# A two-layer hybrid trunk on one core: first loads in quarters, the norm's sum split and moved, and five smaller edits

## The chip, the cores and the metric

The kernel runs on 1 core of one Trainium2 chip. The metric is the device time of that core in microseconds (us). Before the change it is 975.6 us, the median of 3 runs (975.24 to 975.84). TensorE (PE) multiplies, VectorE (DVE) and ScalarE (ACT) move and compute, SyncE (SP) issues most of the transfers. Each engine works through its own list of instructions in order and waits on semaphores for the others.

## What is computed

The input x is 512 tokens by 1024 channels, float32. Two layers follow each other, each of them

```
h = rmsnorm(x, norm_g)
(qa, ka, va, ga, qb, kb, vb, ab, gb, cq, ckv, kr, gc, mg) = split_cols(h @ w_in)
ya = swa_sink_attention(rope(qa), rope(ka), va) * silu(ga)        # window attention, 8 heads, 2 kv heads
log_a = log_sigmoid(ab @ w_alpha + b_alpha) / 16                  # gate of the linear attention, rank 16
yb = rmsnorm(gla_chunk_readout(qb, kb, vb, log_a)) * silu(gb)     # gated linear attention, 4 heads
q_c, kv = rmsnorm(cq) @ w_uq, rmsnorm(ckv) @ w_ukv                # latent attention, 8 heads
yc = mla_attention(q_c, kv, rope(kr)) * silu(gc)
y = sigmoid(mg)[0] * (ya @ w_oa) + sigmoid(mg)[1] * (yb @ w_ob) + sigmoid(mg)[2] * (yc @ w_oc)
x = x + y @ w_out
```

and a last rmsnorm. The norm of h is not applied to x: only its gain is, and the factor rstd, one per token, is multiplied in when a product leaves PSUM.

## The kernel before

**Pieces.** All weights are packed into 77 pieces per layer of 128 x 1024 numbers (512 KB). A piece passes through three slots: SP loads it into `raw`, ACT rounds it to fp32r in `w_hi` (`split_hi`, L861), DVE subtracts and leaves the rest in `w_lo` (`split_lo`, L1152). A product of x with a piece is three passes on PE (L586): hi by hi, hi by the activation's low part, low by hi. A piece of the kind "ring" gives one 128 x 512 bank out of three from 24 such passes of 512 columns; a "natural" piece (`PN1`, pieces 3 to 6, and `PN2`) adds to four banks `nat` in 24 passes of 432 or 512 columns. The first pieces of a layer are 0 (`PX`, the keys of the window attention), 1 and 2 (`PC[0:2]`, cq), 3 to 6 (`PN1`: kb, va, kr, ab), 7 (`PC[2]`, ckv), 8 and 9 (`PQA`).

**The written order.** `make_schedule` makes one list that PE, ACT and DVE all go through in this order, each doing its own part of every step. A piece is four "quarter" steps (quarter q belongs to piece q // 4). ACT does its part at the last quarter of piece p: `split_hi` of piece p + 3, which takes the slot of piece p and so waits until PE has finished p. DVE does `split_lo` of piece p + 2 at the second quarter of piece p. Between the quarters stand named steps:

- `begin`: the last two of eight squares of x on ACT (`square`, L879) and their sums on DVE (`add`, L1127 and L1130). The first six stand ahead of the layer (for layer 0 behind the splits of the first pieces, ahead of everything else). They use `merged` as room: `sq`, `sq_sum`.
- `rms`: PE multiplies `sq_sum` by a matrix of ones in fp32 (L697), ACT takes Ln and Exp (L866, L868; ahead of them it loads its table, L1002), DVE refines it into `rstd` with four instructions (L1135 to L1143) and scales the rotary tables (L1278, L1279). PE waits here for the four constant loads (`setup_loaded`).
- `early`: DVE empties the banks of pieces 0 to 2 (six instructions, L1285 to L1292); ACT squares the two latent tiles (L986), for which it waits on DVE.
- `rstd_nat` (PE transposes rstd, L702; DVE copies, L1314), `lat_sum` (L1296), `rope_k` (DVE, four instructions, L1302 and L1304).
- at the last quarter of piece 6 DVE takes the 48 columns of kr and ab out of `nat` and rotates kr (`k_ab`, L1496 to L1505); `turn_ab` (PE, L708) transposes the result and waits for it.
- `gla_gate`: PE multiplies `ab1` by `alpha_all` (L714), 17 rows (rank 16 and the bias), from partition 32 on; `gla_decay` (L721) is a product of the same width from 128 rows.

The step `latent` sums squares on PE in fp32r, from a hi and a low part (L735, L736), which ACT and DVE make by a copy (L947) and a subtraction (L1320).

In every layer `rms` stands between piece 2 and piece 3, `early` in the middle of piece 3, `rstd_nat` in the middle of piece 4, `rope_k` in the middle of piece 5, `turn_ab` in the middle of piece 7.

**Window attention.** It is worked off in two halves between quarters of output and gate pieces: `score_a` (L783), `divide_a`, `turn_a` (PE transposes, L817, ACT copies out, L1078), then `value_a` (L831) for each of the four tiles of 128 tokens into the bank `aux`, which DVE gates into `y_pre` (L1165) and ACT and DVE split (`y_hi`, `y_lo`). `score_a(1)` needs the banks that ACT empties at `turn_a(0)`; two quarters lie between them. `value_a(2)` and `value_a(3)` have two quarters around each.

**Latent attention.** Piece `PUKV` gives eight banks of 3 passes; ACT empties the even ones, DVE the odd ones (L1542), and behind them DVE does one `split_lo`. Piece `PUQ` gives three banks of 6 passes. DVE waits for two of them, and then rotates them with L1551 to L1554; the second of these frees the first bank.

**The start.** SP loads x tile by tile with the second halves of pieces 0 and 1 in between, then piece 2, the constants (1.2 MB), and piece 3 and on. ACT's queue loads the first quarter of piece 0, `params`, the first half of piece 1 and the second quarter of piece 0 (`HEADS`). PE runs 7 warming products on zeros (L673), and then pieces 0 and 1 together, k by k (`first_pieces`, L660 to L662): k = 0 and 1 of piece 0, the same of piece 1, then both by turns. ACT splits x (L895) and the parts of the pieces (L902, L913), DVE makes the low parts (L1177, L1182).

Of the kernel before, what the change touches and what calls it, by code (L numbers as in the profile page):

```python
# [17 lines left out]
F32 = mybir.dt.float32  # L18
# [33 lines left out]
WARM = 7  # L52
# [51 lines left out]
def make_schedule():  # L104
# [98 lines left out]
    for y in range(2):  # L203
# [87 lines left out]
def build_hybrid_trunk(nc, x_t, pieces, params, alpha, tables, consts, final_g, out_t, k_rope_dram):  # L291
    with ExitStack() as ctx:
# [85 lines left out]
        o_t = o_bank[:, :].rearrange("p (f n) -> p f n", f=BR)  # L378

# [5 lines left out]
        HEADS = ((0, slice(0, 256)), (1, slice(0, 512)), (0, slice(256, 512)))  # L385
        head_loaded = [sig(f"head_loaded{n}", 0) for n in range(3)]
# [14 lines left out]
        warm_set = sig("warm_set", 0)  # L401
        act_used = sig("act_used", 3, 3)
# [50 lines left out]
        def _(sp):  # L453
            for j in range(KT):
                sp.dma_start(xt[:, j, :], x_t[:, j, :]).then_inc(x_loaded[j].sem, 16)
                if j in (3, 4):
                    sp.dma_start(raw[:, j - 3, 512:1024], pieces[j - 3, :, 512:1024]).then_inc(raw_loaded[j - 3].sem, 16)
            sp.dma_start(raw[:, 2, :], pieces[2]).then_inc(raw_loaded[2].sem, 16)
            sp.dma_start(rope[:, :, :], tables).then_inc(setup_loaded.sem, 16)
            sp.dma_start(con[:, :], consts).then_inc(setup_loaded.sem, 16)  # L460
            sp.dma_start(alpha_all[32:32 + B_RANK + 1, :, :], alpha).then_inc(setup_loaded.sem, 16)
            sp.dma_start(fin_g[:, :], final_g).then_inc(setup_loaded.sem, 16)
            for n in range(RAW, DEPTH * PIECES):
# [41 lines left out]
        def _(pe):  # L505
# [140 lines left out]
            def first_pieces():  # L646

                jobs = [(p, k) for p in range(2) for k in range(2)] + [(p, k) for k in range(2, KT) for p in range(2)]
                for p, k in jobs:
                    if k == 0:  # L650
                        pe.wait_ge(proj_free.sem, proj_free.at(0, p - 2))
                        pe.wait_ge(head_lo.sem, p + 1)
                    elif (p, k) == (0, 2):
                        pe.wait_ge(head_lo.sem, 3)
# [4 lines left out]
                    hi, lo = w_hi[:, p, k * P:(k + 1) * P], w_lo[:, p, k * P:(k + 1) * P]  # L659
                    pe.matmul(ring[p][:, :], hi, act_hi[:, k, :], start=k == 0, stop=False)  # L660
# [1023 lines left out]
```

## Time and profile before

| | |
|---|---|
| time, median of 3 runs | 975.6 us (975.24 to 975.84) |
| the profiled execution: its own time | 975.85 us |
| its span in the trace | 974.0 us |
| PE busy | 963.5 us, 99% |
| DVE busy | 578.0 us, 59% |
| ACT busy | 402.5 us, 41% |
| chain that ended last | PE 91%, DVE 5%, ACT 3% |
| granted TensorE clock, mean | 0.999 |

A row of the timeline gives the start, the duration, the engine, the line, the operation, its operands (out<-in) and the count; in brackets stands how long the engine had sat idle and what ended that. Products overlap: a pass of 512 columns lasts 0.39 us in its row, and the next starts 0.227 us after it, so PE's time is read from one start to the next. The same holds for DVE and ACT, where an instruction that waits for nothing can start up to 0.1 us before the end that the row ahead of it gives.

### The profile page before, as it was taken

The numbers are of one execution on the slowest core, as the hardware profiler recorded it, in microseconds if no ns is written. First come the engines' busy times: TensorE is split into PE (matmuls) and PEld (weight loads), VectorE is DVE, ScalarE is ACT, GpSimd is POOL, SyncE is SP. The second block draws the span as 40 slices with busy tenths as digits, with TensorE's granted clock in tenths as the row PEclk, the third lists the DMA queues.
The fourth block names the chain that finished last, engine by engine and source line by source line (L and its number), as shares of the span: only waits on it lengthen the run. The fifth ranks groups of instructions, "written<-read, shape, count | busy, mean of one in ns | idle before, by whom it ended". The sixth has DMA issues, their size and how long they took to land.

```text
span 974.0 us, 13475 instructions
## 1 busy us (share of the span) xinstructions
PE 963.5 (99%) x5440; PEld 787.7 (81%) x5440; DVE 578.0 (59%) x944; ACT 402.5 (41%) x766; POOL 0.9 (0%) x5
## 2 busy tenths in 40 slices
PE   8999999999999999999999999999999999999997
PEld 6878888888888877788888888888888887777887
DVE  6856466346647565665556654744574666665844
ACT  6443343225533354532435324431363424544334
POOL 0000000000000000000000000000000000000000
PEclk9999999999999999999999999999999999999999
DMA  7324313322125221122223333233222341111212
GB/s 269 121 78 139 109 65 109 108 87 87 66 66 161 87 66 66 45 85 88 92 82 108 121 102 115 75 98 104 73 76 93 103 128 66 66 63 47 94 59 87
DMA packets 29968, 91.38 MB, mean 94 GB/s; under 512 B 4353, under 2 KB 6913, under 8 KB 29778
## 3 DMA queue, kind: packets, MB, share of 16 engines
q1 hardware_dynamic: 28770, 89.25, 27.4%
q10 hardware_dynamic: 1136, 1.27, 0.5%
q8 instruction: 43, 0.70, 0.3%
q14 instruction: 19, 0.16, 0.0%
HBM read 84.67 MB, written 2.23 MB: 89 GB/s over the span
## 4 chain that ended last, share of the span: by engine, by line
PE 91%; DVE 5%; ACT 3%; DMA 1%; issue 1%; ACTq 0%; DVEq 0%
PE ring L586 72%; PE nat L586 5%; PE nat L803 3%; PE aux L845 2%; PE nat L810 2%; DVE w_lo L1152 1%; ACT work L1058 1%; PE aux L831 1%; DMA raw<-pieces 1%; ACT w_hi L861 1%; PE nat L783 0%; PE ring L607 0%; PE nat L714 0%; PE ring L608 0%; PE ring L609 0%
## 5 line engine op out<-in xcount | busy, mean ns | idle before, releaser
L586 PE MATMUL ring<-act_hi,w_hi 128*128 128x512 f32 x832 | 330.3, 397 | 0.0
L586 PE MATMUL ring<-act_hi,w_lo 128*128 128x512 f32 x832 | 324.4, 390 | 0.0
L586 PE MATMUL ring<-act_lo,w_hi 128*128 128x512 f32 x832 | 324.2, 390 | 0.0
L861 ACT ACTIVATE w_hi<-raw 128x1024 fp32r<-128x1024 f32 x152 | 161.2, 1062 | 390.4 <-PE ring L586 359.4
L1152 DVE TENSOR_TENSOR w_lo<-raw,w_hi 128x1024 fp32r<-128x1024 f32 x152 | 185.2, 1220 | 50.9 <-ACT w_hi L861 50.9
L586 PEld LDWEIGHTS ring<-act_hi,w_hi 128*128 128x128 f32 x832 | 156.2, 188 | 37.3 <-issue 6.3
L586 PEld LDWEIGHTS ring<-act_hi,w_lo 128*128 128x128 f32 x832 | 156.2, 188 | 33.3
L586 PEld LDWEIGHTS ring<-act_lo,w_hi 128*128 128x128 f32 x832 | 156.3, 188 | 30.5
L1474 DVE SCALAR_TENSOR_TENSOR gates<-ring,rstd 128x512 f32<-128x512 f32 x72 | 49.7, 691 | 140.8 <-PE ring L586 140.8
L586 PE MATMUL ring<-y_hi,w_lo 128*128 128x512 f32 x192 | 74.7, 389 | 0.0
L586 PE MATMUL ring<-y_lo,w_hi 128*128 128x512 f32 x192 | 74.7, 389 | 0.0
L586 PE MATMUL ring<-y_hi,w_hi 128*128 128x512 f32 x192 | 74.7, 389 | 0.0
L586 PE MATMUL nat<-w_hi,act_hi 128*128 128x512 f32 (+1 forms) x128 | 48.8, 381 | 0.4 <-DVE w_lo L1152 0.3
L999 ACT ACTIVATE gates<-gates 128x512 f32<-128x512 f32 x72 | 44.8, 623 | 10.1 <-DVE gates L1474 10.1
L586 PE MATMUL nat<-w_lo,act_hi 128*128 128x512 f32 (+1 forms) x128 | 47.8, 374 | 0.0
L586 PE MATMUL nat<-w_hi,act_lo 128*128 128x512 f32 (+1 forms) x128 | 47.8, 373 | 0.0
L1070 ACT ACTIVATE work<-nat,neg_top 128x128 f32<-128x128 f32 (+3 forms) x64 | 32.9, 526 | 34.9 <-DVE neg_top L1422 34.9
L586 PEld LDWEIGHTS ring<-y_hi,w_hi 128*128 128x128 f32 x192 | 36.0, 188 | 7.5
L586 PEld LDWEIGHTS ring<-y_lo,w_hi 128*128 128x128 f32 x192 | 36.0, 188 | 7.5
L586 PEld LDWEIGHTS ring<-y_hi,w_lo 128*128 128x128 f32 x192 | 36.0, 188 | 7.4
L1524 DVE SCALAR_TENSOR_TENSOR gates<-gates,ring 128x512 f32<-128x512 f32 x32 | 22.0, 687 | 14.8 <-PE ring L586 14.8
L803 PE MATMUL nat<-bank_g,bank_a 32*128 32x128 f32 (+3 forms) x384 | 30.4, 445 | 0.0
(219 smaller groups left out, 998.9 us busy)
## 6 DMA issues: line engine op xcount, KB each, us to landing
raw<-pieces SPq DMA_DIRECT2D x152, 512.0 KB, 3.5
xt<-x_t SPq DMA_DIRECT2D x8, 256.0 KB, 6.9
bank_a<-work SPq DMA_DIRECT2D x32, 64.0 KB, 2.0
out_t<-gates SPq DMA_DIRECT2D x7, 256.0 KB, 2.3
rope<-tables SPq DMA_DIRECT2D x1, 1024.0 KB
bank_a<-work SPq DMA_DIRECT2D x32, 32.0 KB, 2.0
raw<-pieces SPq DMA_DIRECT2D x2, 256.0 KB, 7.3
bank_g<-k_rope_dram SPq DMA_DIRECT2D x8, 64.0 KB, 3.2
```

The source lines that it names most:

```text
L586: mm = pe.matmul(dst, stationary, moving, start=start and i == 0, stop=stop and i == 2)
L803: mm = pe.matmul(nat[a][:, 0:n], q, k, start=part == 0, stop=part == 2)
L810: mm = pe.transpose(nat[a][:, b * P:(b + 1) * P], prob[a][:, b * P:(b + 1) * P], ident)
L831: mm = pe.matmul(o_t[r * 64:r * 64 + 64, 2 * h:2 * h + 2, c * 64:c * 64 + 64], (v_as, v_a)[c][:, i, h * A_DH:(h + 1) * A_DH], pt[:, r, c], ...
L845: mm = pe.matmul(o_t[r * 64:r * 64 + 64, f, :], v_c[:, b, h * C_V:(h + 1) * C_V], prob_t[h % 4][:, b * P:(b + 1) * P], start=b == 0, stop= ...
L861: nc.scalar.activation(w_hi[:, n % HL, :], raw[:, n % RAW, :], ACT.Copy).then_inc(hi_split.sem, 1)
L999: nc.scalar.activation(gates[:, j if j >= 4 else 8 + j, :], gates[:, j, :], ACT.Tanh).then_inc(gate_tanh.sem, 1)
L1058: one = nc.scalar.activation(prob[k][:, hh * P:(hh + 1) * P], nat[k][:, hh * P:(hh + 1) * P], ACT.Exp, scale=A_SCALE, bias=neg_top[:, qt % ...
L1070: nc.scalar.activation(prob[a][:, 0:n], nat[a][:, 0:n], ACT.Exp, scale=C_SCALE, bias=neg_top[:, i % 2, a:a + 1], accum_out=sums[:, qt, 4 * ...
L1152: nc.vector.tensor_tensor(w_lo[:, n % HL, :], raw[:, n % RAW, :], w_hi[:, n % HL, :].bitcast(F32), ALU.subtract).then_inc(lo_split.sem, 1)
L1474: nc.vector.scalar_tensor_tensor(gates[:, j, :], res, 0.5, rstd[:, :], ALU.mult, ALU.mult).then_inc(proj_free.sem, 1)
L1524: nc.vector.scalar_tensor_tensor(merged[:, j, :] if b == 0 else tile, tile, 1.0, z, ALU.add, ALU.mult).then_inc(proj_free.sem, 1)
```

## The change

- **Start.** `WARM` goes from 7 to 4. The first halves of pieces 0 and 1 are loaded in four quarters (`HEADS`): two on ACT's queue behind `params`, two on SP's behind the third tile of x. ACT's wait for `params` moves behind the first split. In `first_pieces` the three passes of a k are ordered hi by hi, low by hi, hi by low activation, each with its own wait ahead of it. SP loads piece 3 ahead of the constants, behind a wait for the low part of piece 0.
- **Squares.** In layer 0 all eight squares and sums stand behind the splits of piece 3 (ACT: last quarter of piece 0; DVE: second quarter of piece 1).
- **rms.** It moves from behind piece 2 to behind piece 3, in both layers; `early`, `rstd_nat`, `lat_sum` move on by about a piece; `rope_k` moves by half a piece only; `turn_ab` and `gla_gate` stay. The sum is taken in fp32r: ACT copies `sq_sum` to `lat_hi[:, 1]`, DVE subtracts into `lat_lo[:, 1]`, PE makes two passes in place of the fp32 product.
- **alpha.** `alpha_all` and `ab1` have all 128 rows, zeros in the rows without a weight; its load grows from 34 KB to 256 KB.
- **Window attention.** Three quarters in place of two behind `turn_a(0)`. The values of tiles 2 and 3 are one step, `values_a`, the second into `nat[0]`; `gate_a` gates them one after the other.
- **Latent attention.** DVE's `split_lo` of `PUKV` stands behind its first copy in place of behind its last; in `PUQ` DVE starts on the first bank before it waits for the second.

```diff
-WARM = 7
+WARM = 4
     piece(PX, PC[0], PC[1])
+    piece(PN1[0])
     step(("rms", 0))
-    half(PN1[0], 0)
+    half(PN1[1], 0)
     step(("early", 0))
-    half(PN1[0], 1)
-    half(PN1[1], 0)
-    step(("rstd_nat", 0), ("lat_sum", 0))
     half(PN1[1], 1)
     half(PN1[2], 0)
+    step(("rstd_nat", 0), ("lat_sum", 0))
+    half(PN1[2], 1)
     step(("rope_k", 0))
-    half(PN1[2], 1)
     piece(PN1[3])
     half(PC[2], 0)
     step(("turn_ab", 0))
...
-        quarters(2 - y)
+        quarters(3 - 2 * y)
     todo.append(("y_hi", 1))
     quarters(1)
+    todo.append(("y_lo", 1))
+    todo.append(("values_a", 2))
     for y in range(2, TT):
-        todo.append(("y_lo", y - 1))
-        todo.append(("value_a", y))
+        todo.append(("gate_a", y))
         quarters(1)
         todo.append(("y_hi", y))
         quarters(1)
-    todo.append(("y_lo", TT - 1))
+        todo.append(("y_lo", y))
...
-        HEADS = ((0, slice(0, 256)), (1, slice(0, 512)), (0, slice(256, 512)))
+        HEADS = ((0, slice(0, 256)), (1, slice(0, 256)), (0, slice(256, 512)), (1, slice(256, 512)))
...
                 sp.dma_start(xt[:, j, :], x_t[:, j, :]).then_inc(x_loaded[j].sem, 16)
-                if j in (3, 4):
+                if j == 2:
+                    for n in range(2, 4):
+                        p, cols = HEADS[n]
+                        sp.dma_start(raw[:, p, cols], pieces[p, :, cols]).then_inc(head_loaded[n].sem, 16)
+                elif j in (3, 4):
                     sp.dma_start(raw[:, j - 3, 512:1024], pieces[j - 3, :, 512:1024]).then_inc(raw_loaded[j - 3].sem, 16)
             sp.dma_start(raw[:, 2, :], pieces[2]).then_inc(raw_loaded[2].sem, 16)
+            sp.wait_ge(lo_split.sem, 1)
+            sp.dma_start(raw[:, 0, :], pieces[RAW]).then_inc(raw_loaded[0].sem, 16)
             sp.dma_start(rope[:, :, :], tables).then_inc(setup_loaded.sem, 16)
             sp.dma_start(con[:, :], consts).then_inc(setup_loaded.sem, 16)
-            sp.dma_start(alpha_all[32:32 + B_RANK + 1, :, :], alpha).then_inc(setup_loaded.sem, 16)
+            sp.dma_start(alpha_all[:, :, :], alpha).then_inc(setup_loaded.sem, 16)
...
                     if k == 0:
                         pe.wait_ge(proj_free.sem, proj_free.at(0, p - 2))
+                        pe.wait_ge(head_hi.sem, p + 1)
+                    elif k == 2:
+                        pe.wait_ge(head_hi.sem, p + 3)
+                    elif k == KT // 2:
+                        pe.wait_ge(hi_split.sem, hi_split.at(0, p + 1))
+                    if p == 0:
+                        pe.wait_ge(x_hi.sem, x_hi.at(0, k + 1))
+                    hi, lo = w_hi[:, p, k * P:(k + 1) * P], w_lo[:, p, k * P:(k + 1) * P]
+                    pe.matmul(ring[p][:, :], hi, act_hi[:, k, :], start=k == 0, stop=False)
+                    if k == 0:
                         pe.wait_ge(head_lo.sem, p + 1)
...
+                    pe.matmul(ring[p][:, :], lo, act_hi[:, k, :], start=False, stop=False)
                     if p == 0:
                         pe.wait_ge(x_lo.sem, x_lo.at(0, k + 1))
-                    pe.matmul(ring[p][:, :], hi, act_hi[:, k, :], start=k == 0, stop=False)
-                    pe.matmul(ring[p][:, :], hi, act_lo[:, k, :], start=False, stop=False)
-                    mm = pe.matmul(ring[p][:, :], lo, act_hi[:, k, :], start=False, stop=k == KT - 1)
+                    mm = pe.matmul(ring[p][:, :], hi, act_lo[:, k, :], start=False, stop=k == KT - 1)
...
# PE, rms
-                        pe.wait_ge(x_acc.sem, x_acc.at(layer, LATE))
-                        mm = pe.matmul(aux[:, :], ones, sq_sum, start=True, stop=True)
+                        pe.wait_ge(sum_lo.sem, sum_lo.at(layer, 1))
+                        pe.matmul(aux[:, :], ones_r[:, :], lat_hi[:, 1, :], start=True, stop=False)
+                        mm = pe.matmul(aux[:, :], ones_r[:, :], lat_lo[:, 1, :], start=False, stop=True)
# PE, gla_gate
-                            mm = pe.matmul(nat_gate[:, t, :], ab1[32:32 + B_RANK + 1, t * P:(t + 1) * P],
-                                           alpha_all[32:32 + B_RANK + 1, layer, :], start=True, stop=True)
+                            mm = pe.matmul(nat_gate[:, t, :], ab1[:, t * P:(t + 1) * P], alpha_all[:, layer, :],
+                                           start=True, stop=True)
# PE
+                    elif name == "values_a":
+                        pe.wait_ge(turn_out.sem, turn_out.at(layer, 8))
+                        pe.wait_ge(o_read.sem, o_read.at(layer, i))
+                        value_a(i, o_t).then_inc(value_done.sem, 1)
+                        value_a(i + 1, o_t2).then_inc(value_done.sem, 1)
# ACT, quarters
+                        if (layer, p) == (0, PX):
+                            first_squares()
# ACT, rms
+                        act.wait_ge(x_acc.sem, x_acc.at(layer, LATE))
+                        nc.scalar.activation(lat_hi[:, 1, :], sq_sum, ACT.Copy).then_inc(sum_hi.sem, 1)
                         nc.scalar.preload_act_table_set(LN_EXP)
# DVE, rms
+                        dve.wait_ge(sum_hi.sem, sum_hi.at(layer, 1))
+                        nc.vector.tensor_tensor(lat_lo[:, 1, :], sq_sum, lat_hi[:, 1, :].bitcast(F32),
+                                                ALU.subtract).then_inc(sum_lo.sem, 1)
# DVE, quarters
                             split_lo(layer, i // 4 + 2)
+                            if (layer, i) == (0, 5):
+                                first_sums()
# DVE, PUKV and PUQ
-                            split_lo(layer, p + 2)
+                                if o == 1:
+                                    split_lo(layer, p + 2)
...
-                                evacuated(layer, p, 2)
+                                evacuated(layer, p, 1)
                                 nc.vector.tensor_tensor(work[:, 0, :], ra, cos, ALU.mult)
                                 nc.vector.tensor_tensor(work[:, 3, :], ra, sin, ALU.mult).then_inc(proj_free.sem, 1)
+                                evacuated(layer, p, 2)
```

## Rows read from the trace of the kernel before

**Rows 1.** The page, part 1: busy time, share of the span and instructions of TensorE.
```profile
PE 963.5 (99%) x5440; PEld 787.7 (81%) x5440; DVE 578.0 (59%) x944; ACT 402.5 (41%) x766; POOL 0.9 (0%) x5
```
**Rows 2.** The warming line: count, durations min/median/max in ns, first and last start.
```profile
L673 PE MATMUL aux<-merged x14: 379/606/767, 1.7 to 6.3; 128*128 128x256 f32 x14
```
**Rows 3.** The page, part 2: transfer rate of 40 equal slices of the span.
```profile
GB/s 269 121 78 139 109 65 109 108 87 87 66 66 161 87 66 66 45 85 88 92 82 108 121 102 115 75 98 104 73 76 93 103 128 66 66 63 47 94 59 87
```
**Rows 4.** Timeline of PE at the start: start, us, engine, line, operation, [idle before].
```profile
7.31 0.47 PE L660 MATMUL ring<-act_hi,w_hi 128*128 128x512 f32 x1 [0.62 <-DVE act_lo L1177]
...
9.80 0.47 PE L660 MATMUL ring<-act_hi,w_hi 128*128 128x512 f32 x1 [0.86 <-DVE w_lo L1182]
...
19.56 0.39 PE L586 MATMUL ring<-act_hi,w_hi 128*128 128x512 f32 x1
```
**Rows 5.** Timeline of ACT at the start.
```profile
5.35 0.42 ACT L902 ACTIVATE w_hi<-raw 128x256 fp32r<-128x256 f32 x1 [1.43 <-DMA par_all<-params]
5.67 1.32 ACT L895 ACTIVATE act_hi<-xt,par_all 128x512 fp32r<-128x512 f32 x2
8.30 0.63 ACT L902 ACTIVATE w_hi<-raw 128x512 fp32r<-128x512 f32 x1 [1.31 <-DMA raw<-pieces]
```
**Rows 6.** Timeline of PE in layer 1, from rms to turn_ab.
```profile
502.12 1.02 PE L697 MATMUL aux<-merged,ones_r 128*128 128x512 f32 x2
...
503.18 0.35 PE L586 MATMUL nat<-w_hi,act_lo 128*128 128x432 f32 x1
...
510.02 0.49 PE L702 MATMUL aux<-con,rstd 128*128 128x128 f32 x3
...
517.92 0.47 PE L586 MATMUL nat<-w_hi,act_hi 128*128 128x432 f32 x1 [0.26 <-DVE w_lo L1152]
...
525.57 0.49 PE L708 MATMUL aux<-con,gates 128*48 128x128 f32 x3
```
**Rows 7.** Timeline of ACT and DVE: a split, a copy and a subtraction in a row.
```profile
51.92 1.06 ACT L861 ACTIVATE w_hi<-raw 128x1024 fp32r<-128x1024 f32 x1 [1.62 <-PE ring L586]
52.89 0.61 ACT L947 ACTIVATE lat_hi<-merged 128x512 fp32r<-128x512 f32 x1
...
53.53 0.69 DVE L1320 TENSOR_TENSOR lat_lo<-merged,lat_hi 128x512 fp32r<-128x512 f32 x1 [0.97 <-ACT lat_hi L947]
```
**Rows 8.** Timeline: a sum in fp32r on PE and ACT's Ln behind it.
```profile
70.20 0.40 PE L735 MATMUL aux<-lat_hi,ones_r 128*128 128x512 f32 x1
...
70.87 0.69 ACT L866 ACTIVATE merged<-aux,eps 128x512 f32<-128x512 f32 x1 [1.62 <-PE aux L736]
```
**Rows 9.** Timeline of ACT and DVE in layer 1, from the norm's Ln to k_ab.
```profile
504.75 0.69 ACT L866 ACTIVATE merged<-aux,eps 128x512 f32<-128x512 f32 x1
...
506.13 0.69 DVE L1135 TENSOR_TENSOR y_pre<-rstd 128x512 f32<-128x512 f32 x1 [6.88 <-ACT rstd L868]
...
525.21 0.22 DVE L1505 TENSOR_TENSOR gates<-gates 128x64 f32<-128x64 f32 x1
```
**Rows 10.** Timeline of PE around gla_gate.
```profile
51.44 0.39 PE L586 MATMUL ring<-act_hi,w_lo 128*128 128x512 f32 x1
51.76 1.99 PE L714 MATMUL nat<-alpha_all,merged 17*128 17x256 f32 x8
53.68 0.50 PE L586 MATMUL ring<-act_hi,w_hi 128*128 128x512 f32 x1
```
**Rows 11.** Timeline of PE in the window attention.
```profile
239.75 0.34 PE L783 MATMUL nat<-bank_a 64*64 64x128 f32 x4 [0.57 <-ACT bank_a L1078]
...
260.50 0.50 PE L586 MATMUL ring<-act_hi,w_hi 128*128 128x512 f32 x1
...
263.44 0.66 PE L831 MATMUL aux<-work,bank_a 128*64 128x128 f32 x8
```
**Rows 12.** Timeline of DVE and PE at piece PUQ.
```profile
289.91 2.35 DVE L1152 TENSOR_TENSOR w_lo<-raw,w_hi 128x1024 fp32r<-128x1024 f32 x2
...
293.61 0.47 PE L586 MATMUL ring<-lat_hi,w_hi 128*128 128x512 f32 x1 [0.26 <-DVE work L1552]
```

More of the change, by code:

```diff
@@ L667, in aux_bank, with value_a @@
                 pe.wait_ge(aux_free.sem, aux_free.at(layer, u))
+            def value_a(i, bank):
+                for h in range(A_KV):
+                    pt = prob_t[2 * (i % 2) + h].rearrange("p (a r c n) -> p r c a n", a=2, r=2, c=2)
+                    for c in range(2):
+                        for r in range(2):
+                            mm = pe.matmul(bank[r * 64:r * 64 + 64, 2 * h:2 * h + 2, c * 64:c * 64 + 64],
+                                           (v_as, v_a)[c][:, i, h * A_DH:(h + 1) * A_DH], pt[:, r, c], start=True, stop=True)
+                return mm
             pe.wait_ge(warm_set.sem, 1)
@@ L793, in _ @@
                         if i == 0:
+                            pe.wait_ge(o_read.sem, o_read.at(layer, TT))
                             pe.wait_ge(proj_free.sem, proj_free.at(layer, by_dve(first_output(PUQ + 2))))
@@ L879, in square @@
                 nc.scalar.activation(sq[n % 2], xt[:, (n - 1 - LATE) % KT, :], ACT.Square).then_inc(x_sq.sem, 1)
-            for n, (p, cols) in enumerate(HEADS):
+            act.dma_start(par_all[:, :, :], params).then_inc(par_loaded.sem, 16)
+            for n in range(2):
+                p, cols = HEADS[n]
                 act.dma_start(raw[:, p, cols], pieces[p, :, cols]).then_inc(head_loaded[n].sem, 16)
-                if n == 0:
-                    act.dma_start(par_all[:, :, :], params).then_inc(par_loaded.sem, 16)
             nc.scalar.preload_act_table_set(LN_EXP)
-            act.wait_ge(par_loaded.sem, 16)
             def split_x(layer, j):
@@ L914, in _, with first_squares @@
             split_hi(0, 2)
-            for n in range(LATE + 1, LATE + 1 + ACT_TILES):
-                square(-1, n, buffer_used=n > LATE + 2)
+            def first_squares():
+                for n in range(LATE + 1, LATE + 1 + ACT_TILES):
+                    square(-1, n, buffer_used=n > LATE + 2)
+                for n in range(1, LATE + 1):
+                    square(0, n)
             for layer in range(DEPTH):
@@ L920, in _ @@
                     if name == "begin":
-                        for n in range(1, LATE + 1):
-                            square(layer, n)
+                        if layer > 0:
+                            for n in range(1, LATE + 1):
+                                square(layer, n)
                     elif name == "split_x" and layer + 1 < DEPTH:
@@ L1187, in _ @@
                 split_x(0, j)
-                if j == 1:
-                    for n in range(1, 3):
+                if j in (1, 2):
+                    for n in ((1,) if j == 1 else (2, 3)):
                         dve.wait_ge(head_hi.sem, n + 1)
@@ L1195, in _, with first_sums @@
             split_lo(0, 2)
-            for n in range(LATE + 1, KT + 1):
-                tile = n - 1 - LATE
-                if tile < ACT_TILES:
-                    dve.wait_ge(x_sq.sem, tile + 1)
-                else:
-                    dve.wait_ge(x_loaded[tile].sem, 16)
-                    dve.wait_ge(x_acc.sem, x_acc.at(-1, n - 2))
-                    nc.vector.tensor_tensor(sq[n % 2], xt[:, tile, :], xt[:, tile, :], ALU.mult
-                                            ).then_inc(dve_sq.sem, 1)
-                    dve.wait_ge(dve_sq.sem, tile - ACT_TILES + 1)
-                add(-1, n)
+            def first_sums():
+                for n in range(LATE + 1, KT + 1):
+                    tile = n - 1 - LATE
+                    if tile < ACT_TILES:
+                        dve.wait_ge(x_sq.sem, tile + 1)
+                    else:
+                        dve.wait_ge(x_loaded[tile].sem, 16)
+                        dve.wait_ge(x_acc.sem, x_acc.at(-1, n - 2))
+                        nc.vector.tensor_tensor(sq[n % 2], xt[:, tile, :], xt[:, tile, :], ALU.mult
+                                                ).then_inc(dve_sq.sem, 1)
+                        dve.wait_ge(dve_sq.sem, tile - ACT_TILES + 1)
+                    add(-1, n)
+                for n in range(1, LATE + 1):
+                    add_square(0, n)
             def add_half(m):
@@ L1665 @@
         params[:, l, SINKS:SINKS + A_HEADS] = a_sinks[l][None, :]
+    rows = np.zeros((P, DEPTH, B_HEADS * B_DK), x.dtype)
+    rows[32:32 + B_RANK] = w_alpha.transpose(1, 0, 2)
+    rows[32 + B_RANK] = b_alpha
     arrays = {
@@ L1669 @@
         "params": params,
-        "alpha": np.ascontiguousarray(np.concatenate([w_alpha, b_alpha[:, None, :]], axis=1).transpose(1, 0, 2)),
+        "alpha": rows,
         "tables": rotary_tables(),
```

34 lines of the change are left out of this document (16 added, 18 removed).

## The prediction, as put on record before the run

> **What bounds the kernel now.** I read, in this order: the page's busy times, PE's gaps from start to start in the timeline, who ended each gap, and then the timelines of ACT and DVE around the steps that move. The page shows TensorE busy for 963.5 of 974.0 us [rows 1]; the reader is to see that whatever is won or lost must be a gap on PE or a pass on PE. Other engines cost nothing until PE waits for them. So each edit is priced by what PE does at its place: a gap that closes, a pass that goes, or a new wait whose chain through ACT and DVE is longer than the work that PE has in between. The few gaps that the change touches are at the start, 7.31 and 9.80 us [rows 4], at a natural piece behind `early`, 517.92 [rows 6], ahead of `score_a(1)`, 239.75 [rows 11], and in `PUQ`, 293.61 [rows 12].
>
> The sum is made against the profiled execution (975.85 us, span 974.0). The median of the three runs is 975.6, 0.25 less; I take the difference found and add it to the median.
>
> **The rms step, both layers: the largest term.** `rms` now stands behind piece 3. At the last quarter of piece 3 ACT has `split_hi` of piece 6, which takes piece 3's slot and so waits until PE has finished piece 3. Behind it in ACT's list stands the new copy of the sum, then DVE's subtraction, and only then may PE's first pass start; PE has nothing else to do, since its list is in order too. The length of this chain is in the trace piece by piece:
> - from the moment at which PE could start its next pass to ACT's split: the last pass ahead of `gla_gate` starts at 51.44 [rows 10], so the next could at 51.67, and ACT starts at 51.92 [rows 7]: 0.25 us;
> - split, then copy: 52.89 - 51.92 = 0.97; copy, then subtraction: 53.53 - 52.89 = 0.64; subtraction 0.69 [rows 7];
> - DVE's end to PE's start: 525.21 + 0.22 = 525.43 against 525.57 [rows 6, 9]: 0.14.
>
> Together 2.7 us of idle PE per layer. Before, PE needed only DVE's sum here, which was long done. Bounds: 2.3 if a copy can start sooner behind the split, 3.1 if in layer 0 the postponed squares make ACT or DVE late. I find them in time: ten DVE instructions of about 0.7 us [rows 9] are 7 us from the split of piece 3 on, while pieces 2 and 3 take 5.4 and 4.7, and the subtraction is not due before ACT's copy; splits 4 and 5 fit in until then.
>
> **From rms to turn_ab, both layers.** DVE's list between these two is a chain that just fitted before: its last `k_ab` instruction ends at 525.43 and PE's transposes start at 525.57 [rows 6, 9]. Now PE has a piece less between the two, DVE only a split less. Counted from the start S of rms:
> - PE: 525.57 - 502.12 = 23.45 before [rows 6]. A natural piece goes, 24 passes at (510.02 - 503.18) / 35 = 0.195, which is 4.69. The gap at 517.92 goes, 0.26 idle and about 0.15 of slow restart, 0.41. The fp32 product took 503.18 - 502.12 - 0.20 = 0.86; two fp32r passes take 2 x 0.23 = 0.46; 0.40 less. PE is there at S + 17.95.
> - ACT and DVE: Ln starts 70.87 - 70.20 = 0.67 behind S [rows 8], the refinement 506.13 - 504.75 = 1.38 behind Ln, the end of `k_ab` 525.43 - 506.13 = 19.30 behind that [rows 9], less one split of piece weights, 2.35 - 1.22 = 1.13 [rows 12]. With 0.14 to PE: S + 20.36.
>
> So PE stands at `turn_ab` for 2.4 us. DVE's list is in order: `early`, the wait for ACT's squares and split 7, `rope_k`, split 8 all stand ahead of `k_ab`. Bounds 1.9 and 2.9. Behind `turn_ab` all steps keep their distances.
>
> From the end of piece 2 to `turn_ab` it was 23.45; it becomes 4.69 + 2.70 + 20.36 = 27.75: **4.3 us more per layer, 8.6 in all**, with the gain of the shorter sum and of the closed gap already in it.
>
> **The start.** Before, pieces 0 and 1 took from 7.31 to 19.56 [rows 4]: 48 passes at 0.227 are 10.9, the rest is the gap ahead of 9.80 (about 1.0: six passes end near 8.75) and restarts. The first pass waited for act_lo; now it needs only the high part of tile 0, which ACT starts at 5.67 and has by about 6.35 [rows 5]: first pass near 6.45. `params` goes first and the weights' quarter behind it, so that the first split still starts near 5.3, as both together landed then [rows 5]. The gap at 9.80 waited for a half piece that landed at 8.30 [rows 5] as the end of the first 404 KB of its queue (128, 20 and 256); the quarter that takes its place is the end of the first 276 KB. At the rate between the two landings (256 KB in 3 us) that is 6.8, with both splits done near 8.1. By then PE has done five or six passes and stands briefly twice. 42 passes remain from about 8.2: end near 17.75. **1.8 us less.** Bounds: 0.8 (the quarter lands no sooner than 8.0) and 2.6 (no gap behind 6.45). Constants and piece 3, 2 MB, are now issued behind the first low part, at about 11 us; at the 269 GB/s of the first slice [rows 3] they take 7 to 8 us, and rms is at 30.
>
> The three warming products less cost nothing if the clock stays up: they go from a stretch that ended ahead of the first piece, with 0.62 idle behind it [rows 4].
>
> **Alpha.** The entry to `gla_gate` takes 51.76 - 51.44 = 0.32 where 0.23 is usual, and the eight records 53.68 - 51.76 = 1.92 [rows 10]; by the fp32 product of 512 columns in 0.86, four of 256 would take 1.72. A full-height product may save up to 0.29, or nothing; I take 0.2, since both comparisons point the same way. **0.4 less in two layers.** By the Trainium skill (TensorE: Matmul & The Clock Gate, step by step: what each phase is for), loading weights scales with columns while the number of rows does not matter; by that rule alone this edit would give 0 and the time would be 0.4 higher. The trace has the extra 0.09 and 0.20, but not what they come from.
>
> **Window attention.** PE sat 0.57 idle at `score_a(1)`, with the restart 0.65 [rows 11]; one more quarter, six passes or 1.36 us, covers it. 1.3 in two layers (1.1 to 1.3). Joining two value steps takes out one change of tile shape around a run of 12 passes: 263.44 - 260.50 = 2.94 against 12 x 0.227 = 2.72, 0.22 [rows 11], and I add 0.1 for the second step's own entry, an estimate: 0.6 in two layers (0.4 to 0.8). The joined step waits for ACT's four copies of about 0.6, which start during the transposes and have 2.94 us of passes behind these.
>
> **PUQ.** The gap at 293.61 is 0.26 idle, 0.4 with the restart [rows 12]: DVE did two splits (2.35) ahead of emptying the first bank. One of them moves into `PUKV`, where DVE's copies come 1.36 us apart and a copy of 0.6 with a split of 1.13 do not fit into that; the third bank may come 0.15 late. I take 0.25 per layer, **0.5**, between -0.2 and 0.8.
>
> **Sum:** 8.6 - 1.8 - 0.4 - 1.3 - 0.6 - 0.5 = 4.0 us slower: 979.85 against the profiled 975.85, **979.6** as a median. With all ends of the terms together 1.9 to 6.9 us slower, that is 977.5 to 982.5.
>
> **Rivals.**
> - *Only the rms wait counts.* If DVE reaches `k_ab` 2.4 us sooner relative to rms (because ACT's `early` squares stop holding split 7), the turn is hidden: 979.6 - 4.8 = 974.8. For it: the gap at 517.92 shows a split that came late there [rows 6]. Against: `k_ab` ended 0.14 ahead of the transposes, with nothing to spare [rows 6, 9], and the change takes away 4.7 us of PE's work and 1.1 of DVE's.
> - *Both waits are covered, the gains stay: faster.* Place: `rms`. It decides when the copy is done as PE ends piece 3, which would need ACT's split of piece 6 not to wait for piece 3. Then there is no 2.7, and with S earlier but DVE's chain already running, no 2.4: 975.6 - 4.6 - 2 x 0.81 = 969.4. Against: slot 6 mod 3 is slot 3 mod 3.
> - *The clock falls.* With 4 products of 0.71 on average the warming ends near 5 and PE is idle for over a us and patchy until 8.2. Its records run from 767, with a median of 606, down to 379 ns [rows 2], the two levels, 1.2 and 2.4 GHz. Eight passes at the lower one would take 0.2 longer each, 1.6: 981.3. If it also fell behind the stalls of 2.7 and 2.4, up to 6 more. For it: such long gaps do not occur before. Against: after the gap of 0.86 at 9.80 passes ran at full rate [rows 4]. The Trainium skill (TensorE: Matmul & The Clock Gate, what's actually happening) has an idle engine fall to half rate and a busy one return; by that rule short gaps like these would leave the clock up.
>
> **How the numbers follow.** Forecast with both waits: 0.66. Clock rival 0.10. Only the rms wait 0.13. Both covered 0.08, with 0.03 for other mishaps. A measurement of this kernel tells from no change what is over 0.2%, 2 us; 973.65 to 977.55 is "same". Slower: the forecast almost whole and the clock, 0.76; same: the first rival and an edge of the forecast, 0.16; faster 0.08. The forecast alone spans 977.5 to 982.0; the range for 8 in 10 reaches down to the first rival: 974.7 to 982.2.
>
> **What would show it.** PE's row at rms idle for some 2.3 us with DVE's subtraction as its releaser, in both layers; ACT's split of piece 6 and the copy right ahead of it; PE's row at `turn_ab` idle for about 2 us, released by `k_ab`; first piece done near 17.75; no idle at `score_a(1)`. It is wrong if PE passes rms without a gap, or if the first pieces end later than 19.

## The result, and the profile after

| | before | after |
|---|---|---|
| median of 6 runs each, us | 975.72 (975.24 to 976.18) | 980.02 (979.50 to 981.49) |
| profiled execution, own time / span, us | 975.85 / 974.0 | 981.49 / 979.7 |
| PE busy, us | 963.5 | 963.4 |
| end of pieces 0 and 1, us | 19.56 | 19.55 |
| end of piece 2 to `turn_ab`, layer 0 / layer 1, us | 23.47 / 23.46 | 27.83 / 27.84 |
| mean granted clock | 0.999 | 0.997 |

The ratio is 1.0045, 95% interval 1.0035 to 1.0056: slower by 0.35 to 0.56%. The forecast was 979.6.

PE is as busy as before [rows 1]; what the kernel lost is idle time. The first part of after's page, busy time by engine:
```profile
PE 963.4 (98%) x5434; PEld 790.0 (81%) x5434; DVE 579.4 (59%) x947; ACT 403.1 (41%) x769; POOL 0.9 (0%) x5
```
The list of PE's waits of after (line, releaser: us in total, times, longest; the one ahead of the warming is left out) shows where: two waits per layer that before did not have, one for the split of the sum of squares and one for `k_ab`.
```profile
PE aux L724 <- DVE lat_lo L1322: 5.1, 2, 2.5
PE aux L736 <- DVE gates L1556: 3.3, 2, 2.4
...
PE ring L668 <- ACT act_hi L921: 0.9, 1, 0.9
```
**The row norm.** Layer 1 of after, timeline of ACT and DVE, answers to [rows 7, 9]. In order: the split of piece 6, the copy of the sum behind it, a table load, DVE's subtraction, Ln, and the last instruction of `k_ab`.
```profile
509.67 1.06 ACT L888 ACTIVATE w_hi<-raw 128x1024 fp32r<-128x1024 f32 x1 [3.64 <-PE nat L594]
510.64 0.61 ACT L1041 ACTIVATE lat_hi<-merged 128x512 fp32r<-128x512 f32 x1
511.27 1.28 ACT L1042 ACT_TABLE_LOAD   x1
...
511.28 0.69 DVE L1322 TENSOR_TENSOR lat_lo<-merged,lat_hi 128x512 fp32r<-128x512 f32 x1 [3.99 <-ACT lat_hi L1041]
...
512.86 0.69 ACT L893 ACTIVATE merged<-aux,eps 128x512 f32<-128x512 f32 x1 [0.31 <-PE aux L725]
...
532.19 0.22 DVE L1556 TENSOR_TENSOR gates<-gates 128x64 f32<-128x64 f32 x1
```
PE in the same stretch of layer 1, with `turn_ab` of layer 0 as the first line; it answers to [rows 6]:
```profile
52.83 0.60 PE L736 MATMUL aux<-con,gates 128*48 128x128 f32 x4 [2.42 <-DVE gates L1556]
...
509.22 0.36 PE L594 MATMUL nat<-w_lo,act_hi 128*128 128x432 f32 x1
512.12 0.47 PE L724 MATMUL aux<-lat_hi,ones_r 128*128 128x512 f32 x1 [2.54 <-DVE lat_lo L1322]
...
512.85 0.54 PE L594 MATMUL nat<-w_hi,act_lo 128*128 128x432 f32 x1
513.19 0.56 PE L594 MATMUL nat<-w_lo,act_hi 128*128 128x432 f32 x1
...
532.56 0.60 PE L736 MATMUL aux<-con,gates 128*48 128x128 f32 x4 [0.88 <-DVE gates L1556]
```
Read the pairs of starts. From the last pass of piece 3 to the first of the norm it is 512.12 - 509.22 = 2.90, of which the pass itself is 0.195: 2.70 lost. From there to `turn_ab` it is 20.44. Behind the stall the passes of layer 1 start 0.36 apart instead of 0.195: PE runs at the lower of its two levels, 1.2 GHz. The windows of after (us, busy time and number by engine, then the granted clock, DMA share, GB/s) show it as 0.61 for 4 us:
```profile
512.00:516.00 4.00, 3.88 (x12) 3.57 (x13) 1.69 (x3) 1.87 (x3) 0.00 (x0) 0.61 0.00 0
516.00:520.00 4.00, 4.00 (x21) 3.82 (x21) 3.92 (x7) 0.00 (x0) 0.00 (x0) 0.97 0.01 2
```
It costs nothing here: `turn_ab` waits for DVE in any case. The slow passes took 1.5 us more, and the idle time at `turn_ab` is shorter by just that, 0.88 instead of 2.42. So both layers have the same 27.8 between the same two points.

**The start.** PE of after, answers to [rows 4]. The first pass starts 1.0 sooner than before, but the passes start 0.43 apart, and full rate begins only at 11.12.
```profile
6.30 0.76 PE L668 MATMUL ring<-act_hi,w_hi 128*128 128x512 f32 x1 [0.86 <-ACT act_hi L921]
...
10.71 0.58 PE L675 MATMUL ring<-act_hi,w_lo 128*128 128x512 f32 x1
11.12 0.39 PE L678 MATMUL ring<-act_lo,w_hi 128*128 128x512 f32 x1
```
**`gla_gate`** of after, answers to [rows 10]:
```profile
56.04 1.89 PE L742 MATMUL nat<-alpha_all,merged 128*128 128x256 f32 x8
57.57 0.59 PE L594 MATMUL ring<-act_hi,w_hi 128*128 128x512 f32 x1
```
The step from its first product to the next piece takes 1.53, before 1.92; from `turn_ab` to `gla_decay`, whose work is the same otherwise, 13.15 (52.83 to 65.98) against 13.52 (48.47 to 61.99). A short window of the timeline starts its row at the first record that falls into it. So it gives the starts of the second and of the last of the eight, before and then after:
```profile
52.08 1.02 PE L714 MATMUL nat<-alpha_all,merged 17*128 17x256 f32 x4
53.37 0.37 PE L714 MATMUL nat<-alpha_all,merged 17*128 17x256 f32 x1
...
56.25 1.02 PE L742 MATMUL nat<-alpha_all,merged 128*128 128x256 f32 x4
57.54 0.38 PE L742 MATMUL nat<-alpha_all,merged 128*128 128x256 f32 x1
```
From the second record to the last it is 1.29 with 17 rows and 1.29 with 128. The difference is at the two ends of the run of products. From the pass ahead of it to the second record it is 0.64 before (from 51.44) and 0.44 after (from 55.81). From the last record to the second pass behind it, it is 0.64 before (to 54.01) and 0.46 after (to 58.00). Together that is 0.38.

The ledger of the two profiled spans, after less before: +4.36 and +4.38 between piece 2 and `turn_ab`; start 0.0; per layer alpha -0.37, the window quarter -0.65, the joined value step -0.36; `PUQ` -0.36 in layer 0 and nothing in layer 1, where the restart ahead of it still takes 0.25. That is 8.7 - 3.1 = 5.6, and the spans differ by 5.7. The profiled execution of after is the longest of its six, 1.5 over their median. In which place the others are shorter no trace shows. An earlier rise of the clock at the start would give part of it: copy_first and old_order, with the same warming and first loads, reached full rate some 1.5 us sooner and ended the two pieces 0.7 and 0.6 sooner than after. That it was so in the other executions of after is argued only.

### The profile page after: what moved, and what is told of

The parts are those of the page before. It is cut to its first block, busy times and chain, and to the rows that moved or that the text cites. A ratio compares the mean times of both kernels' runs of the same rounds, so it can differ in the third digit from the quotient of the medians.

```text
span 979.7 us, 13470 instructions
## 1 busy us (share of the span) xinstructions
PE 963.4 (98%) x5434; PEld 790.0 (81%) x5434; DVE 579.4 (59%) x947; ACT 403.1 (41%) x769; POOL 0.9 (0%) x5
## 3 DMA queue, kind: packets, MB, share of 16 engines
q1 hardware_dynamic: 29184, 89.74, 27.8%
## 4 chain that ended last, share of the span: by engine, by line
PE 94%; DVE 4%; ACT 1%; issue 1%; DMA 0%; ACTq 0%; DVEq 0%
PE ring L594 74%; PE nat L594 5%; PE nat L832 3%; PE aux L872 2%; PE nat L839 2%; DVE w_lo L1192 1%; PE nat L811 1%; PE nat L846 1%; PE aux L692 1%; PE ring L668 0%; PE ring L675 0%; PE ring L678 0%; ACT w_hi L888 0%; PE ring L615 0%; DMA raw<-pieces 0%
```

## Experiments

The kernels of the first four ran on one chip, beside before at 975.55 (975.23 to 976.66, 15 runs); those of the last three on another, beside before at 975.80 (974.93 to 976.38, 21 runs). Their medians are given with the ratio to before. The measure that tells the theories apart is the stretch from the end of piece 2 to `turn_ab`, read from each timeline. All values are in us:

| kernel | end of pieces 0, 1 | piece 2 to `turn_ab`, layer 0 | layer 1 | median |
|---|---|---|---|---|
| before | 19.56 | 23.47 | 23.46 | 975.7 |
| after | 19.55 | 27.83 | 27.84 | 980.02 |
| warm7 | 18.36 | 28.33 | 27.84 | 980.12 |
| copy_first | 18.83 | 27.03 | 27.02 | 982.47 |
| copy_rope | 19.76 | 24.18 | 24.18 | 973.76 |
| small_four | 20.41 | 23.47 | 23.46 | 972.52 |
| old_order | 18.97 | 26.65 | 25.24 | 977.05 |
| warm4_before | 19.89 | 23.47 | 23.46 | 976.16 |
| best | 17.80 | 23.46 | 23.47 | 971.28 |

**warm7.** After, with the warming of before.
```diff
-WARM = 4
+WARM = 7
```


> The changed kernel with WARM = 7 again, all else as changed. Theory (the clock): with four warming products TensorE stayed at half rate until 11.1 us, eleven passes at 0.43 in place of 0.227; with seven it is at full rate when the first piece starts, so pieces 0 and 1 end near 17.8 us in place of 19.55 and the time falls from 980.0 to about 978.3. Rival (the slow passes come from the order of the passes or from the loads, not from the warming): they stay slow until 11 us, pieces 0 and 1 end near 19.5, 980.0.

Measured 980.12 (979.78 to 981.06), ratio 1.0046 (1.0033 to 1.0059). This is the rival's time, but not for the rival's reason. Timeline of PE:
```profile
7.24 0.58 PE L668 MATMUL ring<-act_hi,w_hi 128*128 128x512 f32 x1
7.66 0.40 PE L675 MATMUL ring<-act_hi,w_lo 128*128 128x512 f32 x1
```
The passes run at full rate from 7.66 on and the two pieces end 1.2 sooner than in after, so the slow passes did cost that much. The first pass is 0.9 later than in after, since the seven products, nearly all of them at the lower level, last until it. Then the stall of 2.54 at the norm took the clock down in layer 0 as well, and here the norm's own two products ran slow: the second starts 0.57 behind the first where after has 0.30, Ln and all behind it come later, and the stretch is 28.33. Of the 1.2 there are 0.7 left: the profiled spans are 979.0 and 979.7. The medians show none of it.

**copy_first.** The copy of the sum and its subtraction become a step of their own ahead of the last quarter of piece 2, so that no split that waits for piece 3 stands before them.
```diff
-    piece(PX, PC[0], PC[1])
+    piece(PX, PC[0])
+    half(PC[1], 0)
+    step(("quarter", 4 * PC[1] + 2), ("sum", 0), ("quarter", 4 * PC[1] + 3))
...
# ACT and DVE: the copy and the subtraction
-                    elif name == "rms":
+                    elif name == "sum":
...
```


> The changed kernel, with the copy and the subtraction of the norm's sum as a step of their own one quarter before the end of piece 2, ahead of ACT's splits of pieces 5 and 6. Theory (the rms wait is ACT's order): in layer 1 TensorE passes rms without idling, in layer 0 it waits 0.7 us for the late squares instead of 2.5; the wait at turn_ab stays at 2.4 us in both layers, counted from rms; 980.0 - 2.7 - 2.0 = 975.3. Rival (what limits is the chain from the norm to turn_ab as a whole and not ACT's order): the idle time only moves from rms to turn_ab, 980.0.

Measured 982.47 (981.07 to 983.08), ratio 1.0066 (1.0052 to 1.0080). That is above both expectations, and above after too, by 2.4 in the medians and by 0.5 in the profiled spans. PE's waits of this kernel:
```profile
PE aux L738 <- DVE gates L1559: 7.0, 2, 3.5
...
PE ring L596 <- DVE w_lo L1195: 0.6, 1, 0.6
PE aux L726 <- DVE lat_lo L1324: 0.6, 1, 0.6
```
The wait at the norm is gone in layer 1 and is 0.6 in layer 0 (before the edit 2.5 in both), and the one at `turn_ab` grew from 2.4 to 3.5. ACT of layer 1 shows what I had not priced; PE's product is there at 509.19:
```profile
509.45 1.06 ACT L890 ACTIVATE w_hi<-raw 128x1024 fp32r<-128x1024 f32 x1 [3.64 <-PE nat L596]
510.53 1.28 ACT L1045 ACT_TABLE_LOAD   x1
511.83 0.69 ACT L895 ACTIVATE merged<-aux,eps 128x512 f32<-128x512 f32 x1
```
In after the split and the table load run beside the stall, and Ln starts 0.74 behind the product. Here both stand between the product and Ln, which starts 2.64 behind it. The end of `k_ab` moves only from 27.69 to 26.9 behind piece 2, so of the 2.7 that leave the norm in layer 1 only 0.8 are kept, and the rest turns into waits further on. Behind the stall of 3.49 the passes start 0.43 apart, with no further wait to absorb it. From `turn_ab` to the end of piece 2 of layer 1 this kernel takes 1.3 more than after (453.20 for 451.89), and from `turn_ab` of layer 1 to the end of the span 1.5 more (448.7 for 447.1). With 0.7 less at the start and 0.8 less in each stretch that is the 0.5 between the profiled spans, 980.2 and 979.7. The medians stand 2.4 apart, and where the other 1.9 lie no trace shows.
```profile
51.30 1.02 PE L738 MATMUL aux<-con,gates 128*48 128x128 f32 x4 [3.49 <-DVE gates L1559]
...
52.54 0.63 PE L596 MATMUL ring<-act_lo,w_hi 128*128 128x512 f32 x1
52.97 0.63 PE L596 MATMUL ring<-act_hi,w_lo 128*128 128x512 f32 x1
```
**copy_rope.** As copy_first, and in addition `rope_k` stands behind `turn_ab`, so that its instructions leave DVE's list ahead of `k_ab`.
```diff
-    step(("rope_k", 0))
     piece(PN1[3])
     half(PC[2], 0)
-    step(("turn_ab", 0))
+    step(("turn_ab", 0), ("rope_k", 0))
...
```


> As copy_first, and rope_k moved behind turn_ab, so that DVE has 2.85 us less ahead of k_ab. Theory (turn_ab waits for DVE's list): no idle at turn_ab, k_ab ends some 0.5 us ahead of the transposes; 975.3 - 4.8 = 970.5. Rival (k_ab waits for something else, for example for piece 6 or for ACT): the wait at turn_ab stays, 975.3.

Measured 973.76 (972.33 to 974.38), ratio 0.9978 (0.9969 to 0.9986). PE's waits:
```profile
PE aux L737 <- DVE gates L1558: 1.3, 2, 0.6
PE ring L595 <- DVE w_lo L1194: 0.6, 1, 0.6
PE aux L725 <- DVE lat_lo L1323: 0.6, 1, 0.6
```
The stretch falls to 24.18. That is 2.85 less than in copy_first, the time of the four instructions that moved (46.85 to 49.70 in layer 0 of after), and 3.7 less than in after, in each layer; the kernel is 6.3 faster than after. DVE's list, which is worked off in order, was what held `turn_ab`. The time is 3.3 above the expectation. The two stretches gave 7.3 where the expectation had 9.5, since `turn_ab` still waits 0.63 and 0.64 and a split of layer 1 0.65, and the two pieces end 0.2 later, at 19.76. The remaining 0.9 is again the difference between profiled executions (7.1 apart) and medians (6.3 apart).

**small_four.** Before, with the four small edits and nothing else: alpha at full height, the window quarter, the joined value step, `PUKV` and `PUQ`.
```diff
-        quarters(2 - y)
+        quarters(3 - 2 * y)
...
+    todo.append(("values_a", 2))
...
-        todo.append(("value_a", y))
+        todo.append(("gate_a", y))
...
-  mm = pe.matmul(nat_gate[:, t, :], ab1[32:32 + B_RANK + 1, ...], alpha_all[32:32 + B_RANK + 1, layer, :], ...)
+  mm = pe.matmul(nat_gate[:, t, :], ab1[:, ...], alpha_all[:, layer, :], ...)
... # and the places of split_lo and evacuated at PUKV and PUQ, as in the change
```


> The kernel before with four of the edits alone: full-height alpha, three quarters behind turn_a(0), the joined value step, and DVE's order at PUKV and PUQ; start, squares, rms and written order as before. Theory: what these gave inside the changed kernel they give here: 0.75 for alpha, 1.3 for the quarter, 0.7 for the joined step, 0.6 to 0.7 for PUQ, 3.4 in all, 972.3. Rival (rows do not matter for the time of a product, as a page of the notes says of weight loads): alpha gives 0, 973.1.

Measured 972.52 (972.34 to 973.23), ratio 0.9967 (0.9955 to 0.9980): the sum of the four small terms, 2.8 in the forecast, is 3.0 here. From `turn_ab` of layer 0 on, this kernel is 3.46 shorter than before. Its profiled start, whose code is that of before, is 0.85 longer, since ACT gets the first half of piece 1 only at 9.14 where before has 8.30 [rows 5]. Alpha gives its 0.37 here as well: from `turn_ab` to `gla_decay` it is 13.14 in both layers, 13.52 before. In the window attention PE goes without idle time into `score_a(1)`, where before had 0.57 [rows 11]:
```profile
240.62 0.39 PE L588 MATMUL ring<-act_hi,w_lo 128*128 128x512 f32 x1
240.94 1.98 PE L796 MATMUL nat<-bank_a 64*64 64x128 f32 x64
242.85 1.09 PE L678 MATMUL aux<-work,bank_a 128*64 128x128 f32 x16
```
**old_order.** After, with the written order of the first stage and the place of the squares as before; the split sum stays.
```diff
     piece(PX, PC[0], PC[1])
-    piece(PN1[0])
     step(("rms", 0))
+    half(PN1[0], 0)
+    step(("early", 0))
+    half(PN1[0], 1)
     half(PN1[1], 0)
-    step(("early", 0))
+    step(("rstd_nat", 0), ("lat_sum", 0))
     half(PN1[1], 1)
     half(PN1[2], 0)
-    step(("rstd_nat", 0), ("lat_sum", 0))
+    step(("rope_k", 0))
     half(PN1[2], 1)
-    step(("rope_k", 0))
...
# ACT, DVE: first_squares() and first_sums() ahead of the layer again
```


> The kernel after with one part undone: the written order of the first stage and the place of the first squares are those of the kernel before; the sum of squares is still copied and split for the product of the row norm, and waits for that split. Theory (two waits, each with its own cause): the wait at the row norm's product stays at about 2.5 to 2.7 us in each layer, less some 0.9 for its shorter product; the wait at turn_ab, which the late row norm and the later rope_k made, vanishes, since half of the pieces after it stand before the gate's vectors are asked for. About 976.0 us: 975.55 - 3.4 for the small changes + 2 x (2.7 - 0.8), the start left as after. Rival (the order is innocent; the gate's chain is late whatever the order): turn_ab still waits over 1.5 us in each layer, and the time is 979 or more.

Measured 977.05 (976.26 to 979.37), ratio 1.0012 (1.0003 to 1.0021). PE's waits:
```profile
PE aux L725 <- DVE lat_lo L1323: 5.1, 2, 2.5
PE aux L701 <- DVE ones_r L1210: 1.7, 1, 1.7
...
```
The wait for the split is the same 2.54; the one at `turn_ab` is gone (what else the list has are waits of the start). So each wait has its own cause. In layer 1 the stretch is 25.24, which is 1.78 over before: 2.70 less the 0.9 for the shorter product and the closed gap. Layer 0 has 1.4 more, and this is the clock: behind the same stall the norm's second product starts 0.57 behind the first and the next six passes 0.36 apart, while in layer 1 they are 0.19 apart at once.
```profile
28.10 0.56 PE L595 MATMUL nat<-w_hi,act_hi 128*128 128x432 f32 x1
28.46 0.56 PE L595 MATMUL nat<-w_hi,act_lo 128*128 128x432 f32 x1
...
506.18 0.36 PE L595 MATMUL nat<-w_hi,act_hi 128*128 128x432 f32 x1
506.37 0.35 PE L595 MATMUL nat<-w_hi,act_lo 128*128 128x432 f32 x1
```
With no wait at `turn_ab` behind it, a fallen clock is paid in full.

**warm4_before.** Before, with four warming products.
```diff
-WARM = 7
+WARM = 4
```


> The kernel before with one number changed: 4 warming products instead of 7. Theory (the first passes run at half rate when little work stands before them): the passes of pieces 0 and 1 are 0.43 us apart for longer than before, the end of the two pieces comes later than 19.56 us or at it, and the kernel takes 975.6 to 977.5 us; the clock's rise comes after 8 us. Rival (the warming is idle work; the loads alone set the start): within 0.3 us of before, 975.5, with fast passes from the first.

Measured 976.16 (975.53 to 978.34), ratio 1.0009 (1.0000 to 1.0018). The passes are 0.43 apart until 10.75, nearly as long as in after, but the end of the two pieces comes only 0.33 later than before, since the slow passes fill the gap of [rows 4] in which PE waited for a half piece. The theory's mechanism is there; its price by the medians is 0.36 (0 to 1.8 by the interval), nearly the rival's number. Not every execution came off so well: three of the eleven took 977.7 to 978.3, and none of the 21 of before beside them was over 976.4. On a start whose data come late, a slow clock is nearly free in most executions; on the faster start of after it cost all that the start had won.
```profile
9.89 0.63 PE L660 MATMUL ring<-act_hi,w_hi 128*128 128x512 f32 x1
10.32 0.61 PE L661 MATMUL ring<-act_lo,w_hi 128*128 128x512 f32 x1
...
11.00 0.39 PE L660 MATMUL ring<-act_hi,w_hi 128*128 128x512 f32 x1
```
**best.** What the others point to: the small edits, the new first loads with seven warming products, the order of before, the product in full precision in layer 0, and the split one in layer 1 with the copy made between quarters 6 and 7, far ahead.
```diff
-WARM = 4
+WARM = 7
...
+    half(PC[0], 0)
+    step(("quarter", 4 * PC[0] + 2), ("sum", 0), ("quarter", 4 * PC[0] + 3))
+    piece(PC[1])
     step(("rms", 0))
...
+                        if layer == 0:
...
+                            mm = pe.matmul(aux[:, :], ones, sq_sum, start=True, stop=True)
...
```


> The version that the experiments point to: the four small edits (alpha at full height, the window quarter, the joined value step, PUKV and PUQ), the first loads in quarters with 7 warming products, the written order and the squares' place of before, the row norm's product in full precision in layer 0 and split in layer 1, where the copy and the subtraction stand as their own step between quarters 6 and 7, long before the product. Theory: the gains add up: small_four's 972.5, less 1.2 for the start as the kernel with 7 warming products showed it at the end of pieces 0 and 1, less 0.9 for the shorter product of layer 1: 970.4 us. Rival (a split copy in ACT's queue or the clock takes it back, as it did in copy_first): 972 to 973, no better than the four small edits alone.

Measured 971.28 (970.64 to 971.53), ratio 0.9953 (0.9941 to 0.9966): the fastest, 4.5 below before and 8.7 below after. The warming line (count, durations min/median/max in ns, first and last start), and from PE's timeline its start and its one wait inside the layers:
```profile
L704 PE MATMUL aux<-merged x14: 379/634/767, 1.7 to 6.7; 128*128 128x256 f32 x14
...
6.68 0.58 PE L672 MATMUL ring<-act_hi,w_hi 128*128 128x512 f32 x1
7.10 0.40 PE L679 MATMUL ring<-act_hi,w_lo 128*128 128x512 f32 x1
...
17.80 0.39 PE L598 MATMUL ring<-act_hi,w_hi 128*128 128x512 f32 x1
...
513.42 0.36 PE L598 MATMUL nat<-w_lo,act_hi 128*128 128x432 f32 x1
514.43 0.46 PE L598 MATMUL nat<-w_hi,act_hi 128*128 128x432 f32 x1 [0.66 <-DVE w_lo L1200]
```
The pieces end at 17.80, where the forecast had 17.75. The clock was up before the first pass: the last records of the warming are down to 379 ns. The 0.9 expected for layer 1 is not there: the stretch is 23.47 as before. PE is 0.4 sooner behind the shorter product and waits 0.4 longer at 513.42 for the same split of piece 7, which DVE's list sets. The product was never the end of that stretch.

## Why the prediction was right, and where it was not

- **The wait at the norm: right in size and chain.** Forecast 2.7 per layer, measured 2.70 with 2.54 marked idle. The parts: split to copy 0.97, copy to subtraction 0.64, subtraction to PE 0.84 (0.69 + 0.14 forecast). In layer 0 the postponed squares did not add to it. old_order keeps this wait without the new order; copy_first removes it without the old one.
- **`turn_ab`: right.** Forecast S + 20.36, measured 20.43 and 20.44, and 27.75 from piece 2 against 27.83 and 27.84. The reading that carried it was that `k_ab` ended 0.14 ahead of PE's transposes [rows 6, 9], so nothing PE gave up there could be covered. old_order and copy_rope show the cause from two sides.
- **The start: the step that failed.** Forecast 1.8 less, measured 0.0 in the profiled execution; the pieces ended at 19.55, and the prediction itself had named an end later than 19 as a sign of being wrong. The loads and first splits came in time, and PE waited for none of them behind its first pass, but it worked at the lower level. The term at fault is that the three warming products less would cost nothing. This was the rival of the falling clock, at a price of 1.6; it came true for the start, and best shows the 1.76 with the clock up. I had argued against it from a gap of 0.86 behind which passes ran at full rate [rows 4]. But there the seven products had got PE to its higher level first; the records of the four of after all took 631 ns or more, where those of the seven of before go down to 379 ns [rows 2]. So the three products that were taken out were the ones in which the clock rose. small_four, with seven, even stands idle for 1.97 at 10.64 and runs at full rate behind it.
- **The clock behind the stalls: true but free.** The rival had up to 6 for it. The clock fell behind the wait of 2.54 in one layer of after and not in the other, and what it cost came out of the next wait. The same fall costs 1.4 in old_order.
- **Alpha: 0.37 per layer where the forecast had 0.2.** By the Trainium skill (TensorE: Matmul & The Clock Gate, step by step: what each phase is for) the number of rows should not matter, which would be 0. The traces agree for the products themselves, 1.29 between the same two records with 17 rows and with 128. The gain is at the two ends of the run, 0.20 on entry and 0.18 on exit, where before the 17-row products stood between passes of another shape. The forecast saw 0.09 on entry and 0.20 in the rest, and took 0.2 of the 0.29. What PE does in that time no run shows.
- **Window, joined step, `PUQ`:** forecast 0.65, 0.3 and 0.25 per layer; measured 0.65, 0.36, and 0.36 in one layer with none in the other. The first two are right within 0.1; `PUQ` gave 0.36 in all where the forecast had 0.5.
- **The sum** was 4.0; the spans moved by 5.7 and the medians by 4.3. The difference to the spans is the start's 1.8 and 0.14 of the two stretches, with 0.3 more from the small edits against it. That the median is only 0.4 above the forecast is therefore in part luck: a term of 1.8 failed, and the medians happen to differ by 1.4 less than the profiled spans, a part of which may be executions with a faster start than the profiled one. The width was also worked out wrongly: the ends of all terms, added as the prediction gives them, make 0.7 to 8.3 us slower and not 1.9 to 6.9.
- **Only the rms wait / both covered:** neither. The first would have needed DVE to reach `k_ab` sooner behind the norm. In layer 1 from Ln to the end of `k_ab` it is 20.68 before (504.75 to 525.43) and 19.55 after (512.86 to 532.41), which is the one split less, 1.13, and nothing more.

## What to carry to other kernels

A wait that is taken from PE's list comes back at the next point where PE meets the same in-order queue; price the chain on the other engines from end to end between two fixed points on PE, not the single wait (copy_first took 2.7 out and kept 0.8). Ahead of `turn_ab`, `k_ab` ended only 0.14 us before PE came: so little slack says that no work may be taken from PE there unless as much is taken from DVE. When an edit makes the first work arrive sooner, look at whether PE has reached its higher clock by then; and measure the small edits of a bundle apart from the large ones: here they were worth 3.0 us, while the split sum and its new order cost 8.7.

## What the runs showed of the hardware

- The time at which PE first reached full rate varied by more than the program explains. With four warming products the passes were 0.43 apart until 11.1 in after and copy_rope, 9.6 in old_order, 9.7 in copy_first and 10.8 in warm4_before. With seven, the records of the warming itself became shorter, from 5.2 on in before and from 6.0 on in best, and in warm7 only the last of them did, at 7.2. After and old_order have the same warming, first loads and order of passes. By the Trainium skill (TensorE: Matmul & The Clock Gate, what's actually happening) the monitor behind the gate runs free and is not restarted by a kernel, so the moment varies; these rows agree, and the spread is 1.5 us among the kernels with four products and 2.0 us among those with seven.
- The same stall of 2.54 us was followed by the lower level in layer 1 of after, layer 0 of old_order and both layers of warm7, and not in layer 0 of after or layer 1 of old_order. Behind 3.49 and 3.50 it fell in both layers of copy_first (granted clock 0.73 from 52 to 56 us and 0.57 from 532 to 536). Behind the 1.97 at the start of small_four it did not. The prediction took it that short gaps leave the clock up; for 2.54 us that came true in two cases of six.
- The granted clock of a window at the start reads 1.00 in after from 6.30 to 11.10 while the passes start 0.43 apart. The distance of starts is the safer reading there.
- An ACT table load took 1.28 us and the next activation started 0.02 behind its end (copy_first, 511.83). In after it ran while PE stood still for DVE and cost nothing; in copy_first, where that stall is gone, it stands between PE's product and Ln.
